# Expert results scattered by token and choice, and read back in contiguous tiles

## The reference

```python
pg_top, g_idx = lax.top_k(softmax(h @ rg_w + rg_b), 1)      # one group of 4
pe_top, e_idx = lax.top_k(softmax(el of that group), 2)     # two experts of its 4
gate = pg_top * pe_top / sum(pe_top)
hid = silu(h @ wg[e]) * (h @ wu[e])                          # 1024 -> 256, 16 experts
moe = sum over the two choices of gate * (hid @ wd[e])      # 256 -> 1024
x = x + gate2 * moe
y = rms_norm(x, final_g)
```

## Time and profile before

| | us |
|---|---|
| median of 3 runs | 1419.49 (1418.0 to 1422.6) |
| the profiled execution, its own time | 1422.79 |
| its span in the profile | 1421.2 |
| TensorE busy | 1239.7 |
| VectorE busy | 594.7 |
| ScalarE busy | 415.4 |
| GpSimd busy | 176.8 |

### The profile page before, as it was taken

How to read it: one execution, slowest core, us unless ns; L and a number is a source line. 1 busy time by engine, 2 the same in 40 slices (tenths; PEclk the granted TensorE clock), 3 DMA queues, 4 the chain that set the end, 5 groups by cost and what they waited for, 6 DMA issues and landing times. The chain is left out here.

```text
span 1421.2 us, 28996 instructions
## 1 busy us (share of the span) xinstructions
PE 1239.7 (87%) x10925; PEld 768.8 (54%) x10925; DVE 594.7 (42%) x1007; ACT 415.4 (29%) x856; POOL 176.8 (12%) x384
## 2 busy tenths in 40 slices
PE   5899989999999797899889996899827999999965
PEld 2465465665656565455668886444414555555421
DVE  4300514454555445465545565233461222222227
ACT  3100215565656465341212222011210111111123
POOL 0100101111121333200000000400001110011040
PEclk9999989999999899999989998899957999999988
DMA  9300304101000498465410000801008679856784
GB/s 358 125 0 0 114 15 134 31 16 46 26 21 17 159 405 298 129 205 193 135 20 4 4 4 4 260 32 41 33 13 302 207 248 357 293 161 230 280 315 165
DMA packets 88297, 191.77 MB, mean 135 GB/s; under 512 B 18523, under 2 KB 41570, under 8 KB 82947
## 3 DMA queue, kind: packets, MB, share of 16 engines
q1 hardware_dynamic: 69668, 141.31, 29.1%
q0 software_dynamic: 11376, 37.50, 7.5%
q10 hardware_dynamic: 7152, 11.55, 2.5%
HBM read 163.01 MB, written 27.31 MB: 134 GB/s over the span
## 5 line engine op out<-in xcount | busy, mean ns | idle before, releaser
L2661 PE MATMUL ex_ps_g<-all_mT,ex_xt 128*64 128x256 f32 x1344 | 157.5, 387 | 4.6 <-DMA all_mT<-in_exp_wu 3.2
L1706 PE MATMUL at_ps_p<-all_hT,mix_at_w 128*128 128x363 f32 (+1 forms) x384 | 128.1, 477 | 0.0
L2661 PEld LDWEIGHTS ex_ps_g<-all_mT,ex_xt 128*64 128x64 f32 x1344 | 94.2, 139 | 54.5 <-DMA all_mT<-in_exp_wu 5.6
L2270 PE MATMUL op_ps_o<-all_hT,op_m_t 128*128 128x512 f32 x256 | 114.5, 603 | 7.9 <-POOL op_m_t L2250 7.9
L352 PE MATMUL fr_big<-all_mT,all_hT 128*128 128x256 f32 (+3 forms) x288 | 94.9, 493 | 3.0 <-DVE all_hT L405 3.0
L1706 PEld LDWEIGHTS at_ps_p<-all_hT,mix_at_w 128*128 128x128 f32 x384 | 69.1, 190 | 52.5 <-issue 18.7
L1868 DVE TENSOR_TENSOR_SCAN mix_v_g<-mix_v_g 128x1024 f32<-128x1024 f32 (+3 forms) x32 | 46.8, 1485 | 104.7 <-ACT at_A L1817 80.1
L2680 PE MATMUL ex_ps_y<-all_hT,ex_hid_T 128*64 128x512 f32 x336 | 80.5, 600 | 6.2 <-DMA all_hT<-in_exp_wd 2.9
L2270 PEld LDWEIGHTS op_ps_o<-all_hT,op_m_t 128*128 128x128 f32 x256 | 48.2, 193 | 65.2 <-issue 57.0
L583 PE MATMUL rp_ps<-all_hT,kv_rp_w 128*128 128x384 f32 (+1 forms) x240 | 77.8, 478 | 0.8 <-PEq L1938 0.8
L352 PEld LDWEIGHTS fr_big<-all_mT,all_hT 128*128 128x128 f32 (+1 forms) x288 | 54.1, 188 | 43.2 <-issue 38.2
(11 more groups left out here) (469 smaller groups left out, 2074.2 us busy)
## 6 DMA issues: line engine op xcount, KB each, us to landing
all_mT<-in_exp_wg SPq DMA_DIRECT2D x34, 512.0 KB, 6.0
all_mT<-in_exp_wu SPq DMA_DIRECT2D x34, 512.0 KB, 7.6
all_hT<-in_exp_wd SPq DMA_DIRECT2D x17, 1024.0 KB, 7.8
sa_v<-in_cache_v POOLq DMA_DIRECT2D x64, 256.0 KB, 5.8
rp_w_mod<-in_w_mod SPq DMA_DIRECT2D x16, 1024.0 KB, 5.0
slot_rows<-ex_y ACTq DMA_DIRECT2D x84, 128.0 KB, 5.9
rwkv_R<-in_cache_k SPq DMA_DIRECT2D x32, 256.0 KB, 5.5
rwkv_B<-in_cache_k SPq DMA_DIRECT2D x32, 256.0 KB, 6.3
```

The costliest lines, as they stand in the source:

```text
L1706: last = nc.tensor.matmul(third(j, x_, c), w[:, x_, k, :], hT[:, k, lo:hi], start=(k == 0), stop=(k == KT - 1), skip_group_check=True)
L2270: last = nc.tensor.matmul(ps_o[0:m, u, lo:lo + 512], m_t[:, u, k, 0:m], w[:, k, lo:lo + 512], start=(k == 0), stop=(k == KT - 1))
L2661: final = nc.tensor.matmul(ps_g[rows, u, 0:DE], xt[:, k, HALVES[u]], w1[:, u, x_, k, :], start=(k == 0), stop=(k == KT - 1))
```

## The change

Each result row of a unit is now sent by an indirect DMA of GpSimd (`scatter`) to a place given by its token and choice: `slot_rows` has rows of half the width (2 KB), first a spare area in which every row of every unit has a place of its own, then 2 x 1088 rows for choice 0 and as many for choice 1. The number that the one-hot matmul carries is token + 1, plus 1088 for the second choice, and 0 for an empty row, which goes to its spare place. From it VectorE works out `token` and, in nine further steps (`make_dest`), the places `dest`. ScalarE no longer stores. Each pair of scatters stands behind the gather of two rounds on. SP no longer stores zeros; when all is stored it issues 18 plain loads of contiguous rows, all in the expert block, and GpSimd has nothing to do in `combine`. `gather` copies its indices in one instruction.

```diff
+SPARE_ROWS = EU * P
@@ experts, SP
-                sp.wait_ge(zeros_ready, 1)
-                with sp.Fori(ROUNDS_MIN, ROUNDS) as r:
-                    with sp.If(r > last):
-                        sp.dma_start(slot_rows[bass.ds(r * 2 * UNIT, 2 * UNIT), :], zeros[:, :]).then_inc(zeros_stored, 16)
-                    with sp.Else():
-                        sp.sem_inc(zeros_stored, 16)
-                sp.wait_ge(zeros_stored, (ROUNDS - ROUNDS_MIN) * 16)
+                for u in range(2):
+                    wait_apart(sp, stored[u], last * 16 + 16, s["all_stored"])
+                sp.wait_ge(s["all_stored"], 2)
+                load_rows(sp, keep, slot_rows)
@@ GpSimd
-                nc.gpsimd.iota(token_i[:, :], pattern=[[P, N]], base=0, channel_multiplier=1).then_inc(built, 1)
+                nc.gpsimd.iota(token_i[:, :, :], pattern=[[P, N], [TOK, 2]], base=1, channel_multiplier=1).then_inc(built, 1)
...
+                nc.gpsimd.iota(spare_i[:, :], pattern=[[P, EU]], base=0, channel_multiplier=1).then_inc(built, 1)
...
                 def gather(r):
                     wait_apart(pool, s["turned"], r + 1, s["x_free"])
-                    for u, rows in enumerate(HALVES):
-                        nc.gpsimd.tensor_copy(here[rows, :], token[rows, bass.ds(unit_of(u, r, last), 1)]).then_inc(s["here"], 1)
-                    wait_apart(pool, s["here"], r * 2 + 2, s["x_free"])
+                    nc.gpsimd.tensor_copy(here[:, :], token[:, bass.ds(r, 1)]).then_inc(s["here"], 1)
+                    wait_apart(pool, s["here"], r + 1, s["x_free"])
...
+                def scatter(u, r, count):
+                    wait_apart(pool, s["y_kept"], count, s["y_passed"])
+                    nc.gpsimd.tensor_copy(there[u][:, :], dest[:, bass.ds(unit_of(u, r, last), 1)]).then_inc(s["there"], 1)
+                    wait_apart(pool, s["there"], count, s["y_passed"])
+                    nc.gpsimd.indirect_dma_start(slot_rows, bass.IndirectOffsetOnAxis(ap=there[u][:, 0:1], axis=0),
+                                                 y[:, u, :], None).then_inc(stored[u], 16)
+
                 gather(0)
-                nc.gpsimd.memset(zeros[:, :], 0.0).then_inc(zeros_ready, 1)
-                pool.wait_ge(zeros_ready, 1)
-                rounds(pool, last, 1, gather)
-                gather(last)
-                pool.wait_ge(s["all_stored"], 2)
-                pool.wait_ge(zeros_stored, (ROUNDS - ROUNDS_MIN) * 16)
-                gather_rows(nc, keep, slot_rows, range(GATHERED_FIRST))
+                gather(1)
+                pool.wait_ge(s["dest_made"], 1)
+                with pool.Fori(0, ROUNDS - 2) as r:
+                    with pool.If(last > r + 1):
+                        gather(r + 2)
+                        for u in range(2):
+                            scatter(u, r, r * 2 + u + 3)
+                for u in range(2):
+                    scatter(u, last - 1, last * 2 + u + 1)
+                for u in range(2):
+                    scatter(u, last, last * 2 + u + 3)
@@ ScalarE
                 def back(i, u, r):
                     act.wait_ge(s["down_done"], i + 3)
-                    act.wait_ge(stored[u], r * 32 + 32)
+                    if not (isinstance(r, int) and r == 0):
+                        act.wait_ge(stored[u], r * 16)
                     nc.scalar.activation(y[:, u, :], ps_y[:, u, :], ACT.Copy).then_inc(s["y_kept"], 1)
-                    act.wait_ge(s["y_kept"], i + 3)
-                    for x_, rows in enumerate(HALVES):
-                        act.dma_start(slot_rows[bass.ds(unit_of(u, r, last) * UNIT, UNIT), x_ * (D // 2):(x_ + 1) * (D // 2)],
-                                      y[rows, u, :]).then_inc(stored[u], 16)
@@ VectorE
-                step(V.tensor_copy(slots[:, :], slot_f[:, :]))
...
-                for c in range(2):
-                    mine = unit_token[:, :, :].rearrange("p (n c) u -> p n c u", c=2)[:, :, c, :]
-                    step(V.tensor_tensor(mine, mine, bc(token_f[:, :], 2, EU), ALU.mult))
+                numbers = token_f[:, :, :].rearrange("p n c -> p (n c)")
+                step(V.tensor_tensor(unit_token[:, :, :], unit_token[:, :, :], bc(numbers, 2, EU), ALU.mult))
...
-                V.tensor_copy(token[:, :], ps_tokens).then_inc(s["tokens_kept"], 1)
+                step(V.tensor_scalar(second[:, :], ps_tokens, float(TOK) + 0.5, -float(TOK), ALU.is_gt, ALU.mult))
+                step(V.tensor_tensor(number[:, :], second[:, :], ps_tokens, ALU.add))
+                for rows, units in zip(HALVES, (slice(0, ROUNDS), bass.ds(last + 1, ROUNDS))):
+                    V.tensor_scalar(token[rows, :], number[rows, units], -1.0, 0.0, ALU.add, ALU.max).then_inc(s["tokens_kept"], 1)
...
+                def make_dest():
+                    for half, rows in enumerate(HALVES):
+                        step(V.memset(place_at[rows, :], float(SPARE_ROWS - 2 + half)))
+                    step(V.tensor_copy(spare_f[:, :], spare_i[:, :]))
+                    step(V.tensor_tensor(place_at[:, :], place_at[:, :], spare_f[:, :], ALU.subtract))
+                    step(V.tensor_scalar(held[:, :], number[:, :], 0.5, None, ALU.is_gt))
+                    step(V.tensor_tensor(number[:, :], number[:, :], second[:, :], ALU.subtract))
+                    step(V.scalar_tensor_tensor(place_at[:, :], number[:, :], 2.0, place_at[:, :], ALU.mult, ALU.add))
+                    step(V.tensor_tensor(place_at[:, :], place_at[:, :], held[:, :], ALU.mult))
+                    V.tensor_tensor(dest[:, :], place_at[:, :], spare_f[:, :], ALU.add).then_inc(s["dest_made"], 1)
+
                 keep_x(0)
+                make_dest()
@@ in place of gather_rows
+def load_rows(sp, keep, slot_rows):
+    for n in range(NT + 1):
+        m = rows_of(n)
+        for c in range(2):
+            at = SPARE_ROWS + 2 * (c * TOK + n * P)
+            sp.dma_start(token_rows(keep, n)[0:m, c, :],
+                         slot_rows[at:at + 2 * m, :].rearrange("(t h) d -> t (h d)", h=2)).then_inc(keep["gathered"][n], 16)
@@ combine
-            @block.gpsimd
-            def _(pool):
-                gather_rows(nc, keep, slot_rows, range(GATHERED_FIRST, NT + 1))
```

More of the change, by code:

```diff
@@ L2448, in experts @@
 def experts(nc, T, keep, mod_rows, h2_rows, slot_rows):
-    logits, slots, gates, neg_ones = keep["logits"], keep["slots"], keep["gates"], keep["neg_ones"]
+    logits, gates, neg_ones = keep["logits"], keep["gates"], keep["neg_ones"]
     ident, unit_expert = keep["ident"], keep["expert"]
@@ L2455, in experts @@
     HALVES = [slice(0, UNIT), slice(UNIT, P)]
-    PICKED, PLACED, HOT, EXPERT = 34, 54, 61, 68
+    PICKED, PLACED, HOT, EXPERT = 34, 53, 59, 66
     ROUNDS_MIN = (2 * TOK // UNIT + 1) // 2
@@ L2500, in experts @@
         wd = flat(keep["hT"], 2 * FK * D).rearrange("p (u k d) -> p u k d", u=2, k=FK)
-        token, here = ph.sb("token", [P, EU], U32), ph.sb("here", [P, 1], U32)
+        token, here = ph.sb("token", [P, ROUNDS], U32), ph.sb("here", [P, 1], U32)
+        spare_i, spare_f, place_at = ph.sb("spare_i", [P, EU], I32), ph.sb("spare_f", [P, EU]), ph.sb("place_at", [P, EU])
+        second, number, held = (ph.sb(x_, [P, EU]) for x_ in ("second", "number", "held"))
+        dest, there = ph.sb("dest", [P, EU], U32), [ph.sb(f"there{u}", [P, 1], U32) for u in range(2)]
         x, xt = ph.sb("x", [P, D]), ph.sb("xt", [P, KT, P])
         hid, hid_T = ph.sb("hid", [P, 2, DE]), ph.sb("hid_T", [P, FK, UNIT])
-        y, zeros = ph.sb("y", [P, 2, D // 2]), ph.sb("zeros", [P, D])
-        zeros_ready, zeros_stored = ph.sem("zeros_ready"), ph.sem("zeros_stored")
+        y = ph.sb("y", [P, 2, D // 2])
         ps_x, ps_g = ph.ps("ps_x", [P, KT, P]), ph.ps("ps_g", [P, 2, 2 * DE])
@@ L2512, in experts @@
         names = ("turned x_kept tokens_kept here gu_half gu_done gated upped hid_turned half_kept hid_kept down_done y_kept "
-                 "gathered passed turn_passed x_free all_stored")
+                 "gathered passed turn_passed x_free y_passed all_stored there dest_made")
         s = {x_: ph.sem(x_) for x_ in names.split()}
@@ L2622, in _ @@
-                gather_rows(nc, keep, slot_rows, range(GATHERED_FIRST))
+                pool.sem_inc(s["there"], 2)
+                def scatter(u, r, count):
[4 more added lines that the diff above has]
+                                                 y[:, u, :], None).then_inc(stored[u], 16)
@@ L2624, in _ @@
             @block.tensor
             def _(pe):
-                pe.wait_ge(built, 8)
+                pe.wait_ge(built, 9)
                 pe.wait_ge(did, PICKED)
@@ L2686, in _ @@
                 gate_up(1, 1, 0)
-                pe.wait_ge(s["tokens_kept"], 1)
+                pe.wait_ge(s["tokens_kept"], 2)
                 turn_hidden(0, 0)
@@ L2710, in _ @@
                 act.sem_inc(s["gated"], 2)
-                for u in range(2):
-                    act.sem_inc(stored[u], 32)
                 def front(i, u, r):
```

(17 more changed lines are left out.)

15 lines of the change are left out of this document (7 added, 8 removed).

## The result

| | before | after |
|---|---|---|
| median of 13 runs each, us | 1422.6 (1415.9 to 1426.7) | 1426.93 (1424.4 to 1435.8) |
| ratio, 95% interval | | 1.0049 (1.003 to 1.0069) |
| span of the profiled execution, us | 1421.2 | 1429.9 |

The change makes the kernel 0.49% slower by the ratio, 7.0 us of 1422.6, and its interval lies above 1. The medians differ by 4.3 us only: five of the 13 runs after took 1431.6 to 1435.8 us, at mean granted clocks of TensorE of 0.939 to 0.942 beside 0.945 to 0.949 of the other eight, and they weigh on the ratio more than on the median. The forecast was 1425.2 us, 1421 to 1431, with 0.67 for slower: right in direction, 1.7 us low.

What follows compares the result with a forecast made beforehand. TensorE's pace bounds the expert stage, and the end follows the last stage's first matmul by 51.75 us. Scatter, issues, barrier and gate matrices move that start by +5.7, added to a median of 1419.49: 1425.2 us, range 1421 to 1431.

Steps and rivals of the forecast that it cites:

- 18 loads on SP hold the barrier: At the expert block's end: all engines wait until SP has issued its 18 loads, 9.0 us.
- The term of the issues: SP before the barrier: 18 issues at 0.50 us each, 9.0 us (6.7 to 10.1), no stall.
- the forecast's own signs of being wrong: Barrier passed before SP's last issue, issue much over 0.5 us, scatter landing outside 2.6 to 5.4, TensorE waits changed.
- The rival in which SP's queue fills: SP's loads before the barrier: SP waits for about ten of 18 transfers; +12 us, 1431.5 us; chance 0.07.
- The exposed scatter: After the last result copy: scatter starts at 1360.53, lands 3.3 us later (2.6 to 5.4), SP begins at 1363.9.
- Barrier, table and gate matrices: Between SP's last issue and TensorE's start: barrier 0.16 us, then table load and two gate matrices 2.0 us.
- The start: TensorE's first matmul of the last stage: 1375.1 against 1369.45, +5.7 us (+2.6 to +8.8), with data for every tile.
- What lay behind it, 51.75 us: Last stage: the end comes a fixed 51.75 us after TensorE's first matmul.
- The expert loop, 0: Expert rounds of 12.8 us: scatters fit under TensorE's work, with 2.3 us of cover before the next transpose; 0.
- The late gathers: Rival in the expert loop: gathered rows come too late for transposes; +5 to +7 on the sum, 1431; chance 0.05.
- Start of the stage and zeros: Expert stage's start: small VectorE steps balance, destination steps of 2.1 us lie under a wait, dropped zeros free nobody; 0.
- Loads that don't hold the others: Rival at the barrier: issues cost next to nothing or don't block; -0.9 to -7.0, about 1415 us typically; chance 0.08.

Runs made afterwards that it cites:

- loads alone: Kernel before, with its gathers replaced by 18 plain loads on SP ahead of the barrier, reading other tokens' rows; median 1427.48 us, ratio 1.0048.
- short rows: Changed kernel, but the 16 loads of whole tiles move only 64 of each row's 1024 elements; one run, 1421.47 us.
- eight loads: Changed kernel with the same rows and bytes in 8 DMAs instead of 18, all in the expert block; median 1427.69 us, ratio 1.0065.
- ahead-and-warm kernel: Changed kernel with only tile 0's loads before the barrier, plus 7 and 6 extra TensorE products around the stage change; median 1417.96 us, ratio 1.0005.
- scatters alone: Changed kernel with its scatters, but 18 indirect gathers by GpSimd, four ahead of the barrier, instead of SP's loads; median 1422.02 us, ratio 1.0027.
- first tile ahead: Changed kernel with only tile 0's two loads before the barrier, the other 16 in the combining block; medians 1421.77 and 1418.82 us, ratios 1.0017 and 0.9962.
- all in combine: Changed kernel with all 18 loads at the head of the combining block; median 1422.01 us, ratio 1.0006.

## Why the prediction was right, step by step

*18 loads on SP hold the barrier.* Right, and it is the whole loss: with the loads alone all of it is there, with 16 of them moved none is. *The term of the issues* was mis-sized: 9.0 us was forecast (6.7 to 10.1), 11.34 measured, above the high end, and single issues of up to 1.5 us are one of the forecast's own signs of being wrong. The price of one issue was near right, 0.48 us as the short rows show against 0.50. What was missing is 2.7 us of waiting behind transfers in flight. The rival in which SP's queue fills, given 0.07 and +12 us, was thus partly true; I had taken no stall because 18 transfers of few rows each didn't look like the tiny pieces ahead of the stall at 893.17. The trace of before held a nearer sign in the stretch from which I took the price. There the ninth large load in a row took 1.21 us, where the seven shown singly around it took 0.43 to 0.51:

```profile
6.12 1.21 SPq L242 DMA_DIRECT2D fr_w<-in_w_mod  x1
```

The eight loads show that not the number of DMAs but what is in flight sets this.

*The exposed scatter.* Copy of the indices and gap as forecast (start 1.24 us after the copy's end; 1.17 forecast). The landing was 3.3 us in the sum; SP starts 2.84 us after the scatter's start, so 2.7 to 2.8, near the low end of 2.6. The Trainium skill's line (DMA: Bandwidth & Descriptors, Anatomy of one DMA, SWDGE path) gives an estimate of 2.6 us for the 256 KB. For this store the trace agrees within 0.2 us, while for the gather of the earlier trace rows the page was 1 us low.

*Barrier, table and gate matrices.* From SP's last issue to the table load 0.72 us (0.16 forecast: SP's own drain of 0.37 was not counted), and 2.13 from there to TensorE's first product. Together 2.85 us, where 2.16 was forecast.

*The start.* The terms differ from the forecast by +0.1 (start of the scatter), -0.5 (landing), +2.3 (issues) and +0.7 (barrier to first product), together +2.6: +8.2 instead of +5.7. It was inside the bounds of +2.6 to +8.8. TensorE had data when it came, as forecast.

*What lay behind it, 51.75 us.* 51.2 and 51.7 in the two profiles of after. Two things not in the forecast: VectorE's first row came 6.2 and 6.8 us after TensorE's first product instead of 5.7 to 5.8; and GpSimd's last drain, told below, gave 1.0 back. The first goes with the granted clock of that distance: 5.6 to 5.8 us at 0.66 to 0.68, 6.2 at 0.61, 6.8 at 0.56, and 3.7 at 1.00 in the ahead-and-warm kernel. It doesn't go with how long TensorE was idle before: the scatters alone had 11.2 us of idle time and 6.7 us to the first row, the change 18.9 and 6.2.

*The expert loop, 0.* Not refuted: from stage start to last copy it is 320.5 and 315.8 us after, 321.6, 316.7 and 320.3 before. The second unit's scatter of a round is over before the next transpose:

```profile
1099.39 0.99 POOL L2621 DMA_INDIRECT slot_rows<-ex_y,ex_there  x1 [0.81 <-POOL ex_there L2619]
1101.44 0.96 PEld L2663 LDWEIGHTS ex_ps_x<-all_ident,ex_x 128*128 128x128 f32 x8 [0.39 <-issue]
```

The transposes end at 1102.59, which leaves 2.2 us, as the 2.3 that had been taken as cover. The late gathers did not come. The waits for weights were 6.1, 3.3 and 4.8 us in the profiles of before and 4.7 and 2.0 in those of after; neither a gain nor a loss can be read from that. The profiles spread by 5 us up to the last copy, so a us either way would not be seen.

*Start of the stage and zeros.* The nine steps for the places ran from 1079.5 to 1081.5, and VectorE then still waited for products until 1085.1: covered. The first tile ahead and all in combine leave the zeros out too, and nothing came of that which the other terms don't explain.

*Loads that don't hold the others* fell: 0.48 us per issue against the 0.19 from which it would have decided, and ScalarE stood at the barrier for 16 us.

*The sum in all.* In the first pair of profiles -1.0 up to the last copy (within that stretch's spread), +8.2 for the start, and -0.6 from there to the end (+0.4 ahead of VectorE's first row, -1.0 behind it) make +6.6 us from stage start to end. Over all profiles it is 388.5 - 381.7 = +6.8 us, as the ratio's 7.0. That the two agree so well is partly luck: the 6.8 hold -1.4 of the stretch up to the last copy, which spreads by 5 us. Behind the last copy, where the profiles of one kernel agree within 0.6 us, the change costs 8.2 us.

*The time as a number.* That 1425.2 lies only 1.7 us from 1426.93 is luck in part too. The forecast added 5.7 us to a median of 1419.49 from three runs; the 13 runs of before have 1422.6, 3.1 higher. Against that the forecast would have been 1428.3. The +5.7 lies between the 4.3 of the medians and the 7.0 of the ratio, and errors in it cancel in part: issues taken 2.3 us and the way behind them 0.7 us too cheap, on the other side a landing 0.5 us too dear and a drain of 1.0 us that was not counted.

## What to carry to other kernels

A DMA is issued at the cost of its engine's sequencer, about half a us here, and ahead of a barrier every engine pays for that time: only what the next stage needs first should be issued ahead of it, the rest behind. An estimate of a row of large loads must have two terms, issues times price, and the wait once transfers are in flight; merging the loads here took from the first and gave as much to the second. When runs spread by more than the effect, compare distances inside the profile, from the first changed instruction on, and take a second profile of each kernel before a difference is explained.

## What the runs showed of the hardware

GpSimd's drain at the last barrier depends on what it did in the block. Before, and with the scatters alone, it had issued indirect gathers there, the last some 30 us earlier; after, it had nothing to do. The drain at the barrier behind the last stage, before, with the scatters alone, and after:

```profile
L3062 POOLq DRAIN  x1: 1208/1208/1208, 1418.9 to 1418.9; - x1
```

```profile
L3087 POOLq DRAIN  x1: 1210/1210/1210, 1424.4 to 1424.4; - x1
```

```profile
L3077 POOLq DRAIN  x1: 58/58/58, 1428.7 to 1428.7; - x1
```

All other engines drain in 7 to 19 ns there, so the 1.15 us stands at the end of the kernel and holds them. From VectorE's first row of the last stage to the end of the span it is 46.0 us in the four profiles with gathers in that block, and 44.9 to 45.0 in the nine without. So moving the last stage's gathers off GpSimd is worth 1.0 us, and the forecast had missed it. The loads alone, which is before without the gathers, has 58 ns, and the scatters alone, which is after with them, 1210: so it is the gathers of this block that bring it. Whether a single one is enough wasn't tried.

TensorE's granted clock fell in one profile of a kernel and held in another after the same 2.5 us of waiting (before: 3.42 us at 0.54, and 1.94 us, for the same products). What decides that was not found.
